# A hybrid conv and attention block: the conv groups' sums over partitions moved into the blocks of the next group's transposes

## What is computed

```
h = rms_norm(x, pre_mix_g)
u, gate_b, gate_c, c_q, c_kv, k_rope = split(h @ w_in)
y_conv = gate_b * short_conv_causal(gate_c * u, conv_w)      # 1024 channels, 3 taps
y_conv = group_rms_norm(y_conv, conv_out_g, 8)               # 8 groups of 128 channels
y_attn = group_rms_norm(MLA(c_q, c_kv, k_rope), attn_out_g, 8)
x = x + rms_norm(concat(y_conv, y_attn) @ w_o, post_mix_g)
x = x + rms_norm(relu(rms_norm(x, pre_mlp_g) @ w_up)**2 @ w_down, post_mlp_g)
```

## Time and profile before

| | before |
|---|---|
| time, median of 3 runs (range) | 1095.44 us (1094.99 to 1095.47) |
| the profiled execution: time, span | 1095.19 us, 1093.4 us |
| TensorE (PE) busy | 1079.1 us, 99% |
| VectorE (DVE) busy | 665.4 us, 61% |
| ScalarE (ACT) busy | 512.3 us, 47% |
| mean granted TensorE clock | 0.996 |

### The profile page before, as it was taken

The page is one execution under the profiler, slowest core; times in us unless marked ns, Lnnn a source line. Parts: engine busy times, 40 slices in busy tenths (PEclk is TensorE's granted clock), DMA queues, the critical chain, the costliest instruction groups (busy, mean ns, idle before and its releaser), DMA issues.

```text
span 1093.4 us, 13600 instructions
## 1 busy us (share of the span) xinstructions
PE 1079.1 (99%) x5002; PEld 898.9 (82%) x5002; DVE 665.4 (61%) x707; ACT 512.3 (47%) x654; POOL 98.3 (9%) x108
## 2 busy tenths in 40 slices
PE   9999999999999999999999999999999999999996
PEld 7888888888888788888888888888888888888884
DVE  6465555568974765565565565655656556556566
ACT  6565444455544564444444444444444444444443
POOL 0010121020000620000000000000000000000004
PEclk9999999999999999999999999999999999999998
DMA  9765446444666465566565665655656656566542
GB/s 340 272 212 181 156 157 201 151 156 177 251 218 189 126 213 182 182 192 192 192 192 167 213 187 183 198 175 186 193 187 192 192 192 192 166 214 188 187 167 77
DMA packets 104337, 207.39 MB, mean 190 GB/s; under 512 B 3697, under 2 KB 9457, under 8 KB 103537
## 3 DMA queue, kind: packets, MB, share of 16 engines
q1 hardware_dynamic: 104160, 206.91, 58.0%
q10 hardware_dynamic: 144, 0.04, 0.0%
HBM read 204.84 MB, written 2.10 MB: 189 GB/s over the span
## 4 chain that ended last, share of the span: by engine, by line
PE 95%; DVE 2%; ACT 1%; POOL 1%; DMA 1%; issue 0%; SPq 0%; DVEq 0%; POOLq 0%; ACTq 0%
PE ps L593 30%; PE ps L595 30%; PE ps L594 30%; PE ps L601 3%; DVE w_lo L1146 1%; DMA xT_raw<-in_xT 1%; PE ps L784 0%; PE ps L838 0%; PE ps L789 0%; DVE xT_lo L1349 0%; ACT a_sb L1108 0%; ACT u_sb L972 0%; DVE acc L1378 0%; DVE x_res L1188 0%; DVE acc L1369 0%
## 5 line engine op out<-in xcount | busy, mean ns | idle before, releaser
L1146 DVE TENSOR_TENSOR w_lo<-raw,w_hi 128x1024 fp32r<-128x1024 f32 (+2 forms) x383 | 470.9, 1237 | 375.0 <-ACT w_hi L887 374.3
L887 ACT ACTIVATE w_hi<-raw 128x1024 fp32r<-128x1024 f32 (+2 forms) x383 | 397.2, 1039 | 486.4 <-PE ps L595 479.1
L593 PE MATMUL ps<-w_hi,xT_hi 128*128 128x512 f32 (+1 forms) x800 | 314.5, 393 | 2.2 <-DVE xT_lo L1209 0.9
L595 PE MATMUL ps<-w_lo,xT_hi 128*128 128x512 f32 (+1 forms) x800 | 309.5, 387 | 0.0
L594 PE MATMUL ps<-w_hi,xT_lo 128*128 128x512 f32 (+1 forms) x800 | 309.2, 386 | 0.0
L593 PE MATMUL ps<-w_hi,yT_hi 128*128 128x512 f32 x672 | 263.1, 392 | 0.0
L595 PE MATMUL ps<-w_lo,yT_hi 128*128 128x512 f32 x672 | 261.7, 389 | 0.0
L594 PE MATMUL ps<-w_hi,yT_lo 128*128 128x512 f32 x672 | 261.5, 389 | 0.0
L593 PEld LDWEIGHTS ps<-w_hi,xT_hi 128*128 128x128 f32 x800 | 150.4, 188 | 34.3 <-issue 3.9
L595 PEld LDWEIGHTS ps<-w_lo,xT_hi 128*128 128x128 f32 x800 | 150.3, 188 | 30.7
L594 PEld LDWEIGHTS ps<-w_hi,xT_lo 128*128 128x128 f32 x800 | 150.5, 188 | 28.3
(11 more groups left out here) (143 smaller groups left out, 431.1 us busy)
## 6 DMA issues: line engine op xcount, KB each, us to landing
raw<-in_w_up SPq DMA_DIRECT2D x64, 1024.0 KB, 5.3
raw<-in_w_down SPq DMA_DIRECT2D x64, 1024.0 KB, 5.0
raw<-in_w_in SPq DMA_DIRECT2D x28, 1024.0 KB, 5.2
raw<-in_w_o SPq DMA_DIRECT2D x16, 1024.0 KB, 5.0
raw<-in_w_uq SPq DMA_DIRECT2D x8, 576.0 KB, 3.9
raw<-in_w_ukv SPq DMA_DIRECT2D x4, 1024.0 KB, 5.1
raw<-in_w_in SPq DMA_DIRECT2D x7, 512.0 KB, 8.2
raw<-in_w_in SPq DMA_DIRECT2D x4, 640.0 KB, 8.4
```

The costliest lines, as they stand in the source:

```text
L593: nc.tensor.matmul(dst, x_hi, hi, start=first, stop=False)
L595: mm = nc.tensor.matmul(dst, x_hi, lo, start=False, stop=last)
L887: nc.scalar.activation(w_hi[:, slot, 0:size], raw[:, raw_slot, first:first + size], ACT.Copy).then_inc(hi_ready, 1)
L1146: nc.vector.tensor_tensor(w_lo[:, slot, 0:size], raw[:, raw_slot, first:first + size], f32(w_hi[:, slot, 0:size]), ALU.subtract).then_inc( ...
```

## The change

The plan gets one list of nine subs, `CONV_AT`. At entry i stand conv_norm of group i-1 and, behind it, convT of group i; conv_square of group i stands two subs later. All transposes of conv groups go to bank 7, and each waits until conv_y of the group before is made. All sums go to bank 5, in two halves of 256 columns that alternate; the first two wait for the last pair's probsT copy, which used that bank, the others for the root of two groups before. Nothing is added to or left out of the computation.

```diff
+CONV_AT = [77, 82, 87, 92, 98, 102, 106, 110, 115]
...
-        for c in range(4):
-            for half, t in [(0, 77 + 6 * c), (1, 98 + 4 * c)]:
-                if sub == t:
-                    steps.append(("convT", half, c))
-                if sub == t + 2:
-                    steps.append(("conv_square", half, c))
-                if sub == t + 5:
-                    steps.append(("conv_norm", half, c))
+        for i, t in enumerate(CONV_AT):
+            if sub == t:
+                if i:
+                    steps.append(("conv_norm", (i - 1) // 4, (i - 1) % 4))
+                if i < 8:
+                    steps.append(("convT", i // 4, i % 4))
+            if sub == t + 2 and i < 8:
+                steps.append(("conv_square", i // 4, i % 4))
...
-        def conv_bank(half, c):
-            return 7 if half == 0 else 4 + c
+        CONV_BANK = 7
+
+        def conv_sum(i):
+
+            return ps[:, 5, i % 2 * SEQ:(i % 2 + 1) * SEQ]
...
-                    if a:
-
-                        pe.wait_ge(oT_lo_ready, PAIRS)
-                        if conv_bank(a, b) == conv_bank(0, 0):
-
-                            pe.wait_ge(conv_std_ready, 4)
-                    elif b:
-
-                        pe.wait_ge(conv_std_ready, b)
+                    if a or b:
+
+                        pe.wait_ge(conv_y_ready, 4 * a + b)
                     else:
                         pe.wait_ge(latT_lo_ready, 3)
-                    transposes(conv_bank(a, b), [s[:, a, tb, b * P:(b + 1) * P] for s in (u_sb, b_sb)
+                    transposes(CONV_BANK, [s[:, a, tb, b * P:(b + 1) * P] for s in (u_sb, b_sb)
...
-                    nc.tensor.matmul(ps[:, conv_bank(a, b), 0:SEQ], ones[:], conv_s[:, i % NCONV, :],
+                    if i < 2:
+
+                        pe.wait_ge(probsT0_ready, PAIRS)
+                    else:
+                        pe.wait_ge(conv_std_ready, i - 1)
+                    nc.tensor.matmul(conv_sum(i), ones[:], conv_s[:, i % NCONV, :],
```

## The result

| | before | after |
|---|---|---|
| time, median of 7 runs (range) | 1095.47 us (1094.99 to 1097.43) | 1099.05 us (1098.68 to 1099.30) |
| ratio, 95% interval | | 1.0032 [1.0023, 1.0041] |
| profiled execution: time, span | 1095.19, 1093.4 us | 1098.84, 1097.1 us |
| first conv transposes to last sum | 61.31 us | 64.91 us |

A forecast was written before the change was run, and what follows sets the result against it. TensorE was taken as the bound, with VectorE nearly full where the change moves work. Five waits of 3.85 us less 0.2 us for merging gave 3.6 us, so 1098.8 for the execution, median 1099.0, range 1096.2 to 1101.2 us.

The forecast's parts named there:

- The order on VectorE: At each merged block VectorE makes the 2.98 us norm ahead of the 1.36 us convT, so the square comes late.
- the loop of 7.0 us: Square, w_hi, w_lo, norm, convT take 7.0 us per group against TensorE's 6.35; 0.65 us wait at 106 and at 110.
- b_sb behind the square: At block 98 ScalarE holds square(3) ahead of w_hi and b_sb, which the transposes read; TensorE waits 1.1 us.
- aftermath: Slower products behind a TensorE block, ten at 0.004 us more each, 0.04 us in full; the only thing merging saves.
- stated upper bound of 0.24: Most that six blocks fewer could save on TensorE, 6 x 0.04 us; 0.2 us was taken.
- Banks at nothing: Added waits from bank 7 (conv_y) and bank 5 (square root) cost nothing, covered by the later wait for conv_sq_ready.
- The late weight splits and loads: Later w_hi, w_lo and loads on SyncE do not starve TensorE; costed at nothing, loads up to 1.3 us if uncovered.
- only block 98 waits: Rival, 8%: VectorE's steps overlap better, the loop stays under 6.35 us, b_sb alone is late; 1096.3 us.
- no wait: Rival, 10%: conv_y is ready within TensorE's 6.35 us, so only the merging gain is left; 1095.2 us.
- a real price for switching: Rival, 4%: merging saves a real switch on TensorE; faster than 0.2% needs 2.2 us, 0.37 us per block.
- waits that grow: Rival, 6%: w_hi and raw loads late too, or 0.3 us more at each wait plus 1.3 us of load; about 1101.8 us.
- TensorE's 6.35: TensorE's own distance in us between dense blocks, 0.87 + 5.48, against which the loop on ScalarE and VectorE was set.

The follow-up runs named there:

- e1: Changed kernel with convT of group i listed ahead of conv_norm of group i-1 at each CONV_AT entry; 1095.28 us, ratio 0.9998 to the kernel before.
- e6: Changed kernel with convT listed ahead of conv_norm only from the block at sub 102 on; 1097.26 us, ratio 1.0015 to the kernel before.
- e5: Changed kernel with VectorE's reciprocal taken for only 128 of 256 tokens; 1095.88 us, ratio 1.0006 to the kernel before.
- e7: Changed kernel with VectorE taking the reciprocal three times in each norm; 1124.76 us, ratio 1.0267 to the kernel before.
- e4: Changed kernel with conv_square of group 3 at sub 96 instead of 94, behind b_sb; 1097.92 us, ratio 1.0020 to the kernel before.
- e9: Plan of before with the change's banks, but transposes of groups 4 to 7 in banks 4, 6, 7, 4; 1095.39 us, ratio 0.9996 to before.
- e3: Changed kernel with transposes of groups 4 to 7 in banks 4, 6, 7, 4; 1098.96 us, ratio 1.0032 to the kernel before.
- e2: Plan of before (16 blocks) with the change's banks, transposes in 7 and sums in 5; 1096.01 us, ratio 1.0008 to the kernel before.

## Why the prediction was right

Forecast and measured waits, the latter from starts as above (last product before the block to the second after, less 0.455 us and the block):

| block | forecast | measured |
|---|---|---|
| 92 | 0.25 | 268.95 - 267.28 - 1.33 = 0.34 |
| 98 | 1.1 | 279.10 - 276.67 - 1.33 = 1.10 |
| 102 | 1.2 | 1.14 |
| 106 | 0.65 | 293.57 - 291.58 - 1.33 = 0.66 |
| 110 | 0.65 | 300.56 - 298.59 - 1.33 = 0.64 |
| sum | 3.85 | 3.88 |
| merging (and, in the second figure, banks) | -0.2 | -0.27 to -0.33 |
| total | 3.6 | 3.6 (distance 64.91 - 61.31) |

**The order on VectorE** was the decisive step. e1 and e6 show it, where the order changes, and e5 and e7, where only VectorE's work does. The list at a block reads as forecast, and the loop of 7.0 us is there: the sums of blocks 102, 106 and 110 start at 285.40, 292.40 and 299.39.

**b_sb behind the square** was a second mechanism at its forecast price, 1.1 us. e4 takes it away, and little else changes (0.71 for 0.91 us of idle time at the next block, 0.17 left at this one).

**Merging saves nothing but aftermath.** A merged block without a wait costs 0.87 us, as two alone do. The 0.2 us taken were somewhat small: 0.27 was measured (e9 against e1), and the stated upper bound of 0.24 was passed, so a block leaves a little more behind than 0.04 us.

**Banks at nothing** was right in the changed kernel (e3). Its reason, that conv_sq_ready comes later, is also what limits it: without the merged plan the shared bank costs 0.8 us (e2, e9).

**The late weight splits and loads, costed at nothing,** never held TensorE: from the last sum to the end of the span both kernels take 789.9 us. The square, too, released the sum as forecast, but the profile writes "issue" where I said it would name the square.

**Of the rivals,** "only block 98 waits" fell on the loop being real, "no wait" on the same; a real price for switching fell on e1, which has all blocks merged and gains 0.3 us at most, far from 2.2; "waits that grow" fell on the table above and on the same 789.9 us behind the last sum. The case for "no wait" in the prediction, that before ScalarE waited 3.09 us at a square without TensorE noticing, overlooked how small the margin was: that square ended at 269.51 and its sum started at 270.18, 0.67 us later, and the change puts this sum two subs (2.7 us) earlier.

**Two slips of reading** did no harm. The prediction gives the distances from transposes to sum in the first half as 5, 5, 5 and 6 subs for both kernels; before they are 5 for all four, only after is the last one 6. And it says of 262 to 304 us what the earlier trace rows show from 274 on. The stretch that is missing reads the same:

```profile
262.00:274.00 12.00, 12.00 (x60) 9.99 (x59) 11.53 (x15) 5.71 (x10) 0.00 (x0) 1.00 0.56 214
```

The sum was no luck: the five waits are each within 0.1 us. But the laying out was incomplete in places that show only off the forecast: the bank in the plan of before (e2), TensorE's own order (e6), slack counted twice (e7). The one to remember is e5's: with several loops nearly as long as each other (7.0, 6.6, and TensorE's 6.35) shortening the longest gives back only the difference to the next.

## What to carry to other kernels

When every engine walks one hand-written list, moving a step moves it on all engines: ask for each engine which of the two neighbours in the list the critical engine is waiting for, and put that one first; here two lines in the other order are worth 3.6 us of 1095. An engine at 61% over the span can be full in the stretch that matters, so lay its queue out there with durations of the trace, against the critical engine's own distance between blocks. e1 is the version to keep if the blocks are to be merged: 0.3 us less on TensorE than before (60.98 against 61.31), and in the time no difference that these runs can measure.

## What the runs showed of the hardware

- Merging fp32 blocks among fp32r products saved no switching price: 0.43 us (sum) and 0.44 us (four transposes) alone, 0.87 us together. What remains per block, some 0.045 us (0.27 us over six), lies for the most part in slightly slower products behind it (0.231 us apart instead of 0.227).
- In the changed kernel waits up to 1.15 us left the granted clock at 1.00. So did 2.57 us of idle time in e7 (ahead of the sum at 261.94). Behind e7's longest wait it fell:

```profile
274.83 1.19 PE L841 MATMUL ps<-conv_s,ones 128*128 128x256 f32 x2 [4.44 <-issue]
...
277.11 0.63 PE L598 MATMUL ps<-w_hi,xT_lo 128*128 128x512 f32 x1
277.53 0.63 PE L599 MATMUL ps<-w_lo,xT_hi 128*128 128x512 f32 x1
```

  The two products start 0.42 us apart instead of 0.23, the sum's record is 1.19 us long instead of 0.67, and the mean granted clock of 270 to 280 us is 0.83, so part of it ran at the lower level, 1.2 GHz. The same followed 3.21 us of idle time ahead of the sum at 299.60, and two shorter idle times close together, 1.28 and 1.43 us, ahead of the sum at 286.93 and the transposes at 289.03. It cost nothing in the time there: TensorE was waiting for VectorE anyway, and from block 102 on the sums come 10.56 to 10.57 us apart, the loop of 7.0 us and the 3.55 added to it.
- The Trainium skill's page TensorE: Matmul & The Clock Gate ("HAM oscillation") describes such a return to the lower clock after idle time, and this trace agrees.
